# A diffusion backbone's split matmuls: leading in one weight panel row block by row block instead of two

## The chip, the cores and the metric

The kernel runs on one NeuronCore of a Trainium2 chip, as one program. The metric is the device time of one execution in microseconds (us), as the median of several runs; lower is better. Five engines run side by side, each with its own instruction stream: TensorE (PE, matmuls), VectorE (DVE), ScalarE (ACT), GpSimd (POOL) and SyncE (SP), which here only starts DMA transfers. They wait for each other on semaphores.

## The reference

A backbone of four layers runs over 256 latent tokens and 256 context tokens with 1024 features. Each layer has another token mixer (latent attention, Hyena, S5, FNet), followed by a SwiGLU with 2816 hidden features. Before each of them the stream is normalised and modulated; this gives the matmul's input h. The parts that matter here:

```python
def rmsnorm(x, g):
    xf = x.astype(jnp.float32)
    y = xf * lax.rsqrt(jnp.mean(jnp.square(xf), axis=-1, keepdims=True) + NORM_EPS)
    return (y * g.astype(jnp.float32)).astype(x.dtype)

def modulate(h, shift, scale):
    return h * (1.0 + scale) + shift

def swiglu(h, w13, w2):
    a, b = jnp.split(h @ w13, 2, axis=-1)
    return (jax.nn.silu(a) * b) @ w2
...
    for i in range(DEPTH):
...
        hl = modulate(rmsnorm(xl, mix_pre_g[i]), mod_l[0], mod_l[1])
...
        xl = xl + mod_l[2] * rmsnorm(yl, mix_post_g[i])
        hl = modulate(rmsnorm(xl, ffn_pre_g[i]), mod_l[3], mod_l[4])
        xl = xl + mod_l[5] * rmsnorm(swiglu(hl, ffn_w13[i], ffn_w2[i]), ffn_post_g[i])
```

The first matmul of the attention is `h_lat @ w_in` (1024 to 1088 columns, of which the last 64 are the shared rotary key), the first of Hyena is `h @ w_in` (1024 to 3072). Layers 0 and 1 work on 512 tokens (latent and context), the feed-forwards of layers 2 and 3 on 256.

## The kernel before

**Split matmuls.** Features lie on partitions, in KD = 8 row blocks of 128; tokens lie along the free dimension. To keep accuracy, each operand is split in a rounded part (hi) and a remainder (lo), and `product` issues three matmuls for one block: hi x hi (L935), lo of h x hi of w (L936), hi of h x lo of w (L937). A weight comes in panels of 256 columns, 1 MB each; a panel's two column chunks of 128 are called q = 0 and 1. For one panel and 8 blocks that is 2 x 8 x 3 = 48 matmuls.

**Panels.** `Split` handles them. SP loads panel p into one of two ring slots (`sp_issue`, L213), as soon as panel p - 2 has been split completely. ScalarE rounds a panel in two halves of four blocks (`round`, L892: w_hi <- ring), VectorE forms the remainder of each half (`remain`, L897: w_lo <- ring, w_hi). `nth_split(i, j)` says which count of the semaphore `w_split_ready` means that half j of panel i is there; TensorE waits for it at blocks 0 and 4 (`wait`). w_hi and w_lo hold two panels, so panel 2 overwrites panel 0.

**The join and the lead-in.** Between two stages a `Join` adds the stage's result to the stream x and forms the next input, block by block. VectorE: `normed` (L707), `scaled` (L697, a later block), `update` (L702), `remainder` (L711, which gives h_lo and is the last step of a block). ScalarE between them: shift and scale (L681), rounding to h_hi (L685). A join marked `parts=True` in front of a split matmul knows it as `first`, and does the first panels' rounding and remainders inside its own loop. TensorE follows with `lead_in` (L917): for each block k it waits for h_lo of block k and then multiplies it into all accumulators (PSUM banks) in its list `outs`. Before the change the list has panels 0 and 1, four accumulators of 512 or 256 columns, 12 matmuls for a block; in the attention panel 0 and the 64 rotary columns (panel 1), 9 matmuls. In the middle of the lead-in `w_stepped` tells ScalarE that the first half of w_hi may be overwritten with panel 2.

After the lead-in the panels from 2 on run one after another, panel by panel, each chunk through all eight blocks. Between panels stand pieces of the modulation (`mods.tensor`, L397): matmuls of another weight that is streamed through a ring of two 1 MB slots; SP refills it (L360) in the same queue as the panels.

There are six lead-ins: attention (Mla, from 54 us), feed-forward of layer 0 (468 us), Hyena (872 us), feed-forward of layer 1 (1216 us), and of layers 2 and 3 (2168 and 2446 us, 256 columns). Everything is ordered by hand; no scheduler moves instructions.

## Time and profile before

| | |
|---|---|
| time, median of 3 runs | 2664.7 us (2653.64 to 2664.8) |
| the profiled execution's own time | 2662.34 us |
| its span, first to last instruction | 2660.5 us |
| mean granted TensorE clock | 0.895 of full |
| TensorE busy | 2243.5 us (84%) |
| VectorE busy | 1200.3 us (45%) |
| ScalarE busy | 791.3 us (30%) |
| HBM read | 295.12 MB |

The profile is of one execution. PE stands for matmuls and PEld for weight loads, which overlap them. The recorded length of a matmul includes its way through the array, so that successive ones overlap; what counts is the distance of their starts. The chain is found backwards from the last instruction. A timeline gives start, length, engine, line, operation and tiles (output first), a count, and in brackets how long the engine had stood idle and what ended that.

### The profile page before, as it was taken

To read this page: it belongs to the slowest core of one execution; us is meant where nothing else is said; L and a number is where in the kernel's file an instruction comes from. 1 tells how busy PE (TensorE), PEld (TensorE's weight loads), DVE (VectorE), ACT (ScalarE), POOL (GpSimd) and SP (SyncE) were. 2 spreads that over 40 slices of the span, in tenths; PEclk is the share of its full clock that TensorE was granted. 3 is DMA by queue.
4 is the path that set the end of the run, shared out by engine and by line. 5 is a ranking of instruction groups with operands and counts; after the bars stand their busy time and mean duration, and the time that the engine had idled before them with its cause. 6 is when DMAs were issued, how large, how long until landed. Compare 5 with 4: busy or idle time off the path is not lost.

```text
span 2660.5 us, 31449 instructions
## 1 busy us (share of the span) xinstructions
PE 2243.5 (84%) x13211; PEld 1741.3 (65%) x13211; DVE 1200.3 (45%) x1939; ACT 791.3 (30%) x1293; POOL 169.4 (6%) x139
## 2 busy tenths in 40 slices
PE   4998879999999899898999995352653789988998
PEld 3664446777777675456777774242643779977998
DVE  2223333522333764515322336876576145553554
ACT  2441113422224422124222224110110144443544
POOL 0000000000000001000000001550640000000000
PEclk8997889999999999999999997675665799999999
DMA  6243321343333444213545434010010335532553
GB/s 231 96 166 135 103 79 32 127 139 123 135 138 115 159 159 141 88 48 102 183 159 190 158 127 113 23 26 0 9 32 0 81 122 189 188 106 95 175 189 112
DMA packets 226311, 305.52 MB, mean 115 GB/s; under 512 B 8598, under 2 KB 197729, under 8 KB 225852
## 3 DMA queue, kind: packets, MB, share of 16 engines
q1 hardware_dynamic: 223840, 298.22, 33.2%
q0 software_dynamic: 1616, 5.05, 0.8%
q8 instruction: 104, 1.70, 0.3%
q10 hardware_dynamic: 716, 0.26, 0.0%
q14 instruction: 35, 0.29, 0.0%
HBM read 295.12 MB, written 4.19 MB: 113 GB/s over the span
## 4 chain that ended last, share of the span: by engine, by line
PE 73%; DVE 18%; ACT 4%; DMA 2%; issue 2%; SPq 1%; POOL 0%; DVEq 0%; ACTq 0%
PE bank L935 17%; PE bank L936 16%; PE bank L937 16%; PE bank L397 4%; PE bank L801 3%; PE bank L846 2%; ACT arena L681 2%; PE bank L1653 1%; DVE arena L707 1%; PE bank L2207 1%; PE bank L2209 1%; PE bank L2208 1%; DVE h_lo L711 1%; ACT h_hi L685 1%; PE bank L2167 1%
## 5 line engine op out<-in xcount | busy, mean ns | idle before, releaser
L935 PE MATMUL bank<-h_hi,w_hi 128*128 128x512 f32 (+1 forms) x1480 | 514.6, 348 | 31.6 <-DVE h_lo L711 30.5
L936 PE MATMUL bank<-h_lo,w_hi 128*128 128x512 f32 (+1 forms) x1480 | 506.8, 342 | 0.0
L937 PE MATMUL bank<-h_hi,w_lo 128*128 128x512 f32 (+1 forms) x1480 | 505.5, 342 | 0.0
L897 DVE TENSOR_TENSOR w_lo<-ring,w_hi 128x1024 fp32r<-128x1024 f32 (+1 forms) x282 | 323.6, 1186 | 387.3 <-ACT w_hi L892 387.2
L935 PEld LDWEIGHTS bank<-h_hi,w_hi 128*128 128x128 f32 x1480 | 283.8, 192 | 86.7 <-DVE h_lo L711 41.4
L892 ACT ACTIVATE w_hi<-ring 128x1024 fp32r<-128x1024 f32 (+1 forms) x282 | 274.5, 1019 | 117.0 <-PE bank L937 115.0
L937 PEld LDWEIGHTS bank<-h_hi,w_lo 128*128 128x128 f32 x1480 | 283.8, 192 | 32.4 <-issue 0.2
L936 PEld LDWEIGHTS bank<-h_lo,w_hi 128*128 128x128 f32 x1480 | 283.9, 192 | 29.6 <-issue 0.2
L935 PE MATMUL bank<-g_hi,w_hi 128*128 128x512 f32 (+1 forms) x704 | 241.1, 343 | 0.0
L936 PE MATMUL bank<-g_lo,w_hi 128*128 128x512 f32 (+1 forms) x704 | 237.2, 337 | 0.0
L937 PE MATMUL bank<-g_hi,w_lo 128*128 128x512 f32 (+1 forms) x704 | 236.6, 336 | 0.0
L2207 PE MATMUL bank<-arena 128*128 128x32 f32 x128 | 39.3, 401 | 133.1 <-DVE arena L2127 133.1
L935 PEld LDWEIGHTS bank<-g_hi,w_hi 128*128 128x128 f32 x704 | 133.4, 190 | 26.3 <-issue 10.0
L937 PEld LDWEIGHTS bank<-g_hi,w_lo 128*128 128x128 f32 x704 | 133.6, 190 | 14.3
L936 PEld LDWEIGHTS bank<-g_lo,w_hi 128*128 128x128 f32 x704 | 133.6, 190 | 12.9
L1068 DVE TENSOR_TENSOR arena<-arena,bank 128x512 f32<-128x512 f32 (+1 forms) x88 | 48.3, 553 | 175.3 <-PE bank L937 173.0
L2207 PEld LDWEIGHTS bank<-arena 128*128 128x128 f32 x128 | 34.9, 332 | 133.3 <-issue 133.3
L1049 ACT ACTIVATE g_hi<-arena 128x512 fp32r<-128x512 f32 (+1 forms) x88 | 45.9, 525 | 252.8 <-DVE arena L1068 252.7
L2167 PE MATMUL bank<-ident,arena 128*128 128x128 f32 x128 | 28.6, 398 | 95.3 <-DVE arena L2043 95.3
L1043 ACT ACTIVATE arena<-bank 128x512 f32<-128x512 f32 (+1 forms) x88 | 42.7, 490 | 216.5 <-PE bank L937 215.2
L397 PE MATMUL bank<-mod_ring,silu_c 128*32 128x256 f32 x1408 | 97.8, 399 | 5.5 <-DMA mod_ring<-mod_w 5.5
L2167 PEld LDWEIGHTS bank<-ident,arena 128*128 128x128 f32 x128 | 22.8, 206 | 97.4 <-issue 48.9
(329 smaller groups left out, 3345.8 us busy)
## 6 DMA issues: line engine op xcount, KB each, us to landing
ring<-ffn_w SPq DMA_DIRECT2D x120, 1024.0 KB, 5.1
mod_ring<-mod_w SPq DMA_DIRECT2D x88, 1024.0 KB, 7.2
ring<-ffn_w SPq DMA_DIRECT2D x16, 768.0 KB, 4.4
ring<-hy_w_in SPq DMA_DIRECT2D x12, 1024.0 KB, 5.2
arena<-mod_w SPq DMA_DIRECT2D x8, 1024.0 KB, 17.5
ring<-s_w_glu SPq DMA_DIRECT2D x8, 1024.0 KB, 5.4
ring<-mla_w_uq SPq DMA_DIRECT2D x8, 576.0 KB, 4.2
ring<-mla_w_in SPq DMA_DIRECT2D x4, 1024.0 KB, 7.1
```

Source lines behind the costliest of these rows:

```text
L397: last = nc.tensor.matmul(MODB[32 * g:32 * g + 32, 0:256], silu_c[:, k, :], self.slot(m)[:, kk, 256 * g:256 * g + 256], start=(k == 0), st ...
L681: last = nc.scalar.activation(dst, src, ACT.Identity, bias=mod.shift(f > 1, k, s), scale=mod.factor(f, k, s))
L801: last = nc.tensor.matmul(self.banks[c % 4][:, 0:self.n], v[:, kl, q * P:(q + 1) * P], self.rhs(k), start=(k == 0), stop=(k == self.kk - 1))
L846: last = nc.tensor.matmul(self.bank(c, t)[:, 0:self.n], v[:, k, q * P:(q + 1) * P], self.rhs(k), start=(k == 0), stop=(k == KD - 1))
L892: nc.scalar.activation(self.hi[:, i % SPLIT, a:b], self.w.slot(i)[:, a:b], ACT.Copy).then_inc(w_rounded, 1)
L897: nc.vector.tensor_tensor(self.lo[:, i % SPLIT, a:b], self.w.slot(i)[:, a:b], self.hi[:, i % SPLIT, a:b].bitcast(F32), ALU.subtract).then_ ...
L935: nc.tensor.matmul(o, w[0], v[0], start=first, stop=False)
L936: nc.tensor.matmul(o, w[0], v[1], start=False, stop=False)
L937: return nc.tensor.matmul(o, w[1], v[0], start=False, stop=last)
L1068: nc.vector.tensor_tensor(self.silus[:, q, 0:n], self.silus[:, q, 0:n], self.out(i, q)[:, 0:n], ALU.mult).then_inc(ffn_product, 1)
L2167: last = nc.tensor.transpose(bank[q][:, j * P:(j + 1) * P], self.pw[:, 2 * q + j // 2, j % 2, :], ident[:, :])
L2207: nc.tensor.matmul(o, self.m0[:, gh, :], self.u[:, g, 0:CH], start=True, stop=False)
```

## The change

In each of the six places only panel 0 is led in block by block, over two accumulators (6 matmuls for a block). Panel 1 follows behind the lead-in in the usual order: chunk by chunk, each through all blocks. In the join, VectorE forms panel 1's two remainders no longer behind blocks 0 and 2 but behind block 7, and `nth_split` counts the halves in their plain order. ScalarE's roundings stay where they were. The modulation piece that belongs to panel 1 now stands behind panel 1.

```diff
--- before.py
+++ after.py
@@ -753,12 +753,11 @@
                         update(k + 1)
                     if self.parts:
                         remainder(k)
-                        if k == 0:
-                            self.first.remain(dve, 1, 0)
                         if k == 2:
                             self.first.remain(dve, 0, 1)
+                        if k == KD - 1:
+                            self.first.remain(dve, 1, 0)
                             self.first.remain(dve, 1, 1)
-                        if k == KD - 1:
                             self.first.remain(dve, 2, 0)
 
 
@@ -870,8 +869,6 @@
 
             def nth_split(self, i, j):
 
-                if self.stepped and i < 2:
-                    return 2 * self.s0 + 2 * j + i + 1
                 return 2 * (self.s0 + i) + j + 1
 
             def halves(self, i):
@@ -991,11 +988,10 @@
 
             def tensor(self, pe):
                 n = self.n
-                lead_in(pe, self.w, self.pre, [(i, q, self.out(i, q)[:, 0:n]) for i in range(2) for q in range(2)], ffn_summed)
+                lead_in(pe, self.w, self.pre, [(i, q, self.out(i, q)[:, 0:n]) for i in range(1) for q in range(2)], ffn_summed)
                 mods.tensor(pe, (self, 0))
-                mods.tensor(pe, (self, 1))
                 for i, (kind, part, kk, c) in enumerate(self.plan):
-                    if i < 2:
+                    if i < 1:
                         continue
                     hi, lo = self.w.parts(i)
                     for q in range(2):
@@ -1164,11 +1160,11 @@
                 pool.dma_start(self.turn[0:ROPE], A["k_turn"]).then_inc(self.loaded, 16)
 
             def tensor(self, pe):
-                lead_in(pe, self.win, self.pre, [(0, 0, bank[0][:, :]), (0, 1, bank[1][:, :]), (1, 0, bank[2][0:ROPE, :])], self.z_summed)
-                for n in range(3):
+                lead_in(pe, self.win, self.pre, [(0, 0, bank[0][:, :]), (0, 1, bank[1][:, :])], self.z_summed)
+                for n in range(2):
                     mods.tensor(pe, (self, "in", n))
                 for n, (c, i) in enumerate(zip(self.order, self.panel)):
-                    if n < 3:
+                    if n < 2:
                         continue
                     m = ROPE if c == 8 else P
                     hi, lo = self.win.parts(i)
@@ -1566,10 +1562,9 @@
                     rhs = self.zt[0:EMB, :] if r == 0 else self.a[0:WIDTH, :]
                     nc.tensor.matmul(bank[5][0:WIDTH, 0:LAT], lhs, rhs, start=True, stop=True).then_inc(self.f_summed, 1)
 
-                lead_in(pe, self.win, self.pre, [(c // 2, c % 2, self.out(c)[:, :]) for c in range(4)], self.u_summed)
+                lead_in(pe, self.win, self.pre, [(c // 2, c % 2, self.out(c)[:, :]) for c in range(2)], self.u_summed)
                 mods.tensor(pe, (self, "in", 0))
-                mods.tensor(pe, (self, "in", 1))
-                for c in range(4, 24):
+                for c in range(2, 24):
                     if c in self.SINES:
                         if c == self.SINES[0]:
                             pe.wait_ge(self.u_moved, 6)
```

On TensorE, in the feed-forward of layer 0, around the first block of the lead-in. Before (the banks are the accumulators; h_split_ready is the wait for h_lo of a block):

```order
L935 MATMUL bank1<-h_hi_51,w_hi_52 128x512
L936 MATMUL bank1<-h_lo_56,w_hi_52 128x512
L937 MATMUL bank1<-h_hi_51,w_lo_53 128x512
L935 MATMUL bank2<-h_hi_51,w_hi_52 128x512 [waits w_split_ready]
L936 MATMUL bank2<-h_lo_56,w_hi_52 128x512
L937 MATMUL bank2<-h_hi_51,w_lo_53 128x512
L935 MATMUL bank3<-h_hi_51,w_hi_52 128x512
L936 MATMUL bank3<-h_lo_56,w_hi_52 128x512
L937 MATMUL bank3<-h_hi_51,w_lo_53 128x512
L935 MATMUL bank0<-h_hi_51,w_hi_52 128x512 [waits h_split_ready]
```

and now:

```order
L934 MATMUL bank0<-h_hi_51,w_lo_53 128x512
L932 MATMUL bank1<-h_hi_51,w_hi_52 128x512
L933 MATMUL bank1<-h_lo_56,w_hi_52 128x512
L934 MATMUL bank1<-h_hi_51,w_lo_53 128x512
L932 MATMUL bank0<-h_hi_51,w_hi_52 128x512 [waits h_split_ready]
L933 MATMUL bank0<-h_lo_56,w_hi_52 128x512
L934 MATMUL bank0<-h_hi_51,w_lo_53 128x512
L932 MATMUL bank1<-h_hi_51,w_hi_52 128x512
```

The six matmuls into bank2 and bank3 no longer stand between block 0 and block 1. At the end of the same lead-in TensorE now has, where before bank2 and bank3 of block 7, the modulation and then panel 2 (bank4) stood:

```order
L932 MATMUL bank1<-h_hi_51,w_hi_52 128x512
L933 MATMUL bank1<-h_lo_56,w_hi_52 128x512
L934 MATMUL bank1<-h_hi_51,w_lo_53 128x512
L932 MATMUL bank2<-h_hi_51,w_hi_52 128x512 [waits w_split_ready]
L933 MATMUL bank2<-h_lo_56,w_hi_52 128x512
L934 MATMUL bank2<-h_hi_51,w_lo_53 128x512
L932 MATMUL bank2<-h_hi_51,w_hi_52 128x512
L933 MATMUL bank2<-h_lo_56,w_hi_52 128x512
L934 MATMUL bank2<-h_hi_51,w_lo_53 128x512
```

Panel 1's run into bank2 and then bank3, 48 matmuls, begins behind the last block. On VectorE in the join before that feed-forward, before (w_lo is a weight remainder, h_lo that of a block, arena_50 the join's scratch; the line numbers are those of each file):

```order
L897 TENSOR_TENSOR w_lo_53<-ring,w_hi_52 128x1024 [waits w_rounded]
L711 TENSOR_TENSOR h_lo_56<-arena_50,h_hi_51 128x512 [waits h_rounded]
L897 TENSOR_TENSOR w_lo_53<-ring,w_hi_52 128x1024 [waits w_rounded]
L707 TENSOR_TENSOR arena_50<-x_sb,bank4 128x512 [waits x_updated]
L697 TENSOR_TENSOR arena_50<-arena_50,bank5 128x512
L702 TENSOR_TENSOR x_sb<-x_sb,arena_50 128x512 [waits join_step]
L711 TENSOR_TENSOR h_lo_56<-arena_50,h_hi_51 128x512 [waits h_rounded]
L707 TENSOR_TENSOR arena_50<-x_sb,bank4 128x512 [waits x_updated]
L697 TENSOR_TENSOR arena_50<-arena_50,bank5 128x512
L702 TENSOR_TENSOR x_sb<-x_sb,arena_50 128x512 [waits join_step]
L711 TENSOR_TENSOR h_lo_56<-arena_50,h_hi_51 128x512 [waits h_rounded]
L897 TENSOR_TENSOR w_lo_53<-ring,w_hi_52 128x1024 [waits w_rounded] x2
```

and now:

```order
L894 TENSOR_TENSOR w_lo_53<-ring,w_hi_52 128x1024 [waits w_rounded]
L711 TENSOR_TENSOR h_lo_56<-arena_50,h_hi_51 128x512 [waits h_rounded]
L707 TENSOR_TENSOR arena_50<-x_sb,bank4 128x512 [waits x_updated]
L697 TENSOR_TENSOR arena_50<-arena_50,bank5 128x512
L702 TENSOR_TENSOR x_sb<-x_sb,arena_50 128x512 [waits join_step]
L711 TENSOR_TENSOR h_lo_56<-arena_50,h_hi_51 128x512 [waits h_rounded]
L707 TENSOR_TENSOR arena_50<-x_sb,bank4 128x512 [waits x_updated]
L697 TENSOR_TENSOR arena_50<-arena_50,bank5 128x512
L702 TENSOR_TENSOR x_sb<-x_sb,arena_50 128x512 [waits join_step]
L711 TENSOR_TENSOR h_lo_56<-arena_50,h_hi_51 128x512 [waits h_rounded]
L894 TENSOR_TENSOR w_lo_53<-ring,w_hi_52 128x1024 [waits w_rounded]
L707 TENSOR_TENSOR arena_50<-x_sb,bank4 128x512 [waits x_updated]
```

One weight remainder behind block 0 and one behind block 2 are gone. Behind block 7, before:

```order
L711 TENSOR_TENSOR h_lo_56<-arena_50,h_hi_51 128x512 [waits h_rounded]
L707 TENSOR_TENSOR arena_50<-x_sb,bank4 128x512 [waits x_updated]
L711 TENSOR_TENSOR h_lo_56<-arena_50,h_hi_51 128x512 [waits h_rounded]
L897 TENSOR_TENSOR w_lo_53<-ring,w_hi_52 128x1024 [waits w_rounded] x2
L1068 TENSOR_TENSOR arena_50<-arena_50,bank2 128x512 [waits ffn_silu,ffn_summed]
L1068 TENSOR_TENSOR arena_50<-arena_50,bank3 128x512 [waits ffn_silu,ffn_summed]
L1084 TENSOR_TENSOR g_lo_55<-arena_50,g_hi_54 128x512 [waits ffn_g_rounded] x2
```

and now:

```order
L711 TENSOR_TENSOR h_lo_56<-arena_50,h_hi_51 128x512 [waits h_rounded]
L707 TENSOR_TENSOR arena_50<-x_sb,bank4 128x512 [waits x_updated]
L711 TENSOR_TENSOR h_lo_56<-arena_50,h_hi_51 128x512 [waits h_rounded]
L894 TENSOR_TENSOR w_lo_53<-ring,w_hi_52 128x1024 [waits w_rounded] x4
L1064 TENSOR_TENSOR arena_50<-arena_50,bank2 128x512 [waits ffn_silu,ffn_summed]
L1064 TENSOR_TENSOR arena_50<-arena_50,bank3 128x512 [waits ffn_silu,ffn_summed]
L1080 TENSOR_TENSOR g_lo_55<-arena_50,g_hi_54 128x512 [waits ffn_g_rounded] x2
```

Two more of them stand behind the last h_lo: panel 1's two, ahead of panel 2's first half.

## Rows read from the trace of the kernel before

**Rows 1.** The page: TensorE's busy time and its clock in 40 slices.
```profile
PE 2243.5 (84%) x13211; PEld 1741.3 (65%) x13211; DVE 1200.3 (45%) x1939; ACT 791.3 (30%) x1293; POOL 169.4 (6%) x139
...
PEclk8997889999999999999999997675665799999999
```

**Rows 2.** The page's chain that ended last: by engine, by line.
```profile
PE 73%; DVE 18%; ACT 4%; DMA 2%; issue 2%; SPq 1%; POOL 0%; DVEq 0%; ACTq 0%
PE bank L935 17%; PE bank L936 16%; PE bank L937 16%; PE bank L397 4%; PE bank L801 3%; PE bank L846 2%; ACT arena L681 2%; PE bank L1653 1%; DVE arena L707 1%; PE bank L2207 1%; PE bank L2209 1%; PE bank L2208 1%; DVE h_lo L711 1%; ACT h_hi L685 1%; PE bank L2167 1%
```

**Rows 3.** Waits: who for whom, total us, times, longest.
```profile
PE bank L935 <- DVE h_lo L711: 36.4, 25, 3.9
```

**Rows 4.** Timelines of ScalarE and VectorE, feed-forward 0's lead-in.
```profile
477.81 1.09 ACT L681 ACTIVATE arena<-arena,modv,affine 128x256 f32<-128x256 f32 x2 [3.63 <-DVE arena L707]
...
488.93 0.69 DVE L711 TENSOR_TENSOR h_lo<-arena,h_hi 128x512 fp32r<-128x512 f32 x1 [0.50 <-ACT h_hi L685]
...
492.05 0.69 DVE L711 TENSOR_TENSOR h_lo<-arena,h_hi 128x512 fp32r<-128x512 f32 x1 [1.83 <-ACT h_hi L685]
```

**Rows 5.** Timeline of TensorE, the same lead-in.
```profile
480.34 0.53 PE L935 MATMUL bank<-h_hi,w_hi 128*128 128x512 f32 x1 [2.37 <-DVE h_lo L711]
480.67 0.62 PE L936 MATMUL bank<-h_lo,w_hi 128*128 128x512 f32 x1
...
483.66 0.59 PE L937 MATMUL bank<-h_hi,w_lo 128*128 128x512 f32 x1
...
492.97 0.39 PE L935 MATMUL bank<-h_hi,w_hi 128*128 128x512 f32 x1
...
495.46 0.39 PE L937 MATMUL bank<-h_hi,w_lo 128*128 128x512 f32 x1
```

**Rows 6.** Timelines of SP and TensorE, behind Hyena's lead-in.
```profile
905.07 0.58 SPq L360 DMA_DIRECT2D mod_ring<-mod_w  x1
...
915.98 1.07 PE L397 MATMUL bank<-mod_ring,silu_c 128*32 128x256 f32 x16 [2.81 <-DMA mod_ring<-mod_w]
```

**Rows 7.** Timeline of VectorE, the attention's lead-in.
```profile
53.80 0.42 DVE L897 TENSOR_TENSOR w_lo<-ring,w_hi 128x256 fp32r<-128x256 f32 x1
54.14 0.68 DVE L707 TENSOR_TENSOR arena<-x_sb,bank 128x512 f32<-128x512 f32 x1
```

**Rows 8.** Timelines of VectorE and TensorE, end of feed-forward 2's lead-in.
```profile
2184.04 1.22 DVE L897 TENSOR_TENSOR w_lo<-ring,w_hi 128x1024 fp32r<-128x1024 f32 x1
...
2186.91 0.28 PE L936 MATMUL bank<-h_lo,w_hi 128*128 128x256 f32 x1
2187.03 0.28 PE L937 MATMUL bank<-h_hi,w_lo 128*128 128x256 f32 x1
2187.56 0.39 PE L935 MATMUL bank<-h_hi,w_hi 128*128 128x256 f32 x1 [0.26 <-DVE w_lo L897]
```

**Rows 9.** The chain in order of time, feed-forward 0: start, us, what.
```profile
474.90 2.27 DVE w_lo L897 x2
```

**Rows 10.** SP's timeline and DMA issues (median to landing), feed-forward 2.
```profile
2173.63 1.50 SPq L213 DMA_DIRECT2D ring<-ffn_w  x2
...
ring<-ffn_w SPq DMA_DIRECT2D x2, 1024.0 KB, 6.5
```

**Rows 11.** Busy us by stretch, PE first; behind POOL, the granted clock.
```profile
231.00:405.00 174.00, 139.84 (x651) 81.77 (x652) 70.93 (x215) 28.10 (x98) 0.00 (x0) 0.76 0.29 97
...
480.67:484.08 3.41, 3.41 (x9) 2.63 (x8) 2.88 (x6) 1.78 (x4) 0.00 (x0) 0.50 0.83 277
```

**Rows 12.** Timeline of TensorE: the shortest and longest of the other five pauses.
```profile
2176.66 0.39 PE L935 MATMUL bank<-h_hi,w_hi 128*128 128x256 f32 x1 [1.57 <-DVE h_lo L711]
2176.89 0.28 PE L936 MATMUL bank<-h_lo,w_hi 128*128 128x256 f32 x1
2177.01 0.28 PE L937 MATMUL bank<-h_hi,w_lo 128*128 128x256 f32 x1
...
2455.30 0.39 PE L935 MATMUL bank<-h_hi,w_hi 128*128 128x256 f32 x1 [2.45 <-DVE h_lo L711]
```

## The prediction, written before the changed kernel ran

> **What bounds the kernel now.** I read the page first. TensorE is busy for 84% of the span and its granted clock is full except in a few slices [rows 1]. The chain that ended last runs along TensorE for 73% of the span, and three lines of it, the three products of a split matmul (L935 to L937), hold half of the span alone [rows 2]. So an edit is worth what it does to the moment at which TensorE gets past a place, unless another engine stands in front of TensorE there. The waits say where one does: matmuls of L935 waited 36.4 us for the block remainders of L711 [rows 3]. All of these lie in the six lead-ins, where a stage's activations arrive block by block. Then I read the timelines of the lead-ins, VectorE beside TensorE. In the feed-forward of layer 0, h_lo blocks come 3.12 us apart on VectorE (488.93, then 492.05) [rows 4]. TensorE's twelve matmuls of a block start 0.226 us apart (492.97 to 495.46, eleven steps) and take 2.7 us [rows 5]. So 2.7 of every 3.12 us in the loop are matmul work that has to be done anyway: the lead-in hides it. The last block ends at 492.74 (492.05 plus 0.69) and TensorE takes it at 492.97, so TensorE is 0.2 us behind there, and only 12 matmuls are left.
>
> **The change, part by part.** It touches six places: the lead-ins of the four feed-forwards, of the latent attention and of Hyena.
>
> 1. TensorE. None of its matmuls is added or removed, but six instead of twelve stand between two blocks, and panel 1's 48 follow as one run. Behind the last block stood 12 matmuls, now 6 + 48 = 54: 42 more that used to lie under VectorE's loop. Nothing covers them, since panel 2 stands behind them in TensorE's order. For 512 columns 42 x 0.226 = 9.5 us, plus 0.1 for the slower start of a run behind a wait (480.34 to 480.67 is 0.33): +9.6. For 256 columns the steps are 0.12 (2186.91 to 2187.03) [rows 8]: 42 x 0.12 + 0.1 = +5.1. In the attention panel 1 is one chunk of 64 columns: before 9 matmuls after the last block, now 6 + 24, 21 x 0.228 + 0.1 = +4.9.
>
> 2. VectorE. Two weight remainders leave the loop (behind block 0 and behind block 2) and stand behind block 7. A pair takes 2.27 us on the chain, from start to next start [rows 9], that is 1.14 each. ScalarE waits for VectorE's L707 after both places, behind block 2 for 3.63 us [rows 4], so the loop of the two engines shortens by what VectorE drops: the last block comes 2.27 us earlier. In the attention the two are 128x256, and the next instruction starts 0.34 after one [rows 7]: -0.7. At the end TensorE needs the first of them for panel 1. It starts 0.08 before the block's end, as the pair in the loop does, runs 1.22, and so ends 1.1 us after the block. TensorE's six last matmuls cover that at 512 columns (1.5 us), but not at 256 (0.8 us): +0.3 there. The second one is needed 12 matmuls later, 2.7 or 1.4 us, and is ready.
>
> 3. Waits that panel 1 now covers. In Hyena the third modulation panel waited 2.81 us for its DMA [rows 6]. TensorE comes there 7 us later and the load, issued at 905.07 before, is not later, since SP waits for panel 2's remainder, which GpSimd's setup (it waits for the last h_lo) and not panel 1 sets: -2.8. In the narrow feed-forwards panel 2's fifth block waited for its remainder: it started 0.53 after its forerunner instead of 0.12 [rows 8]: -0.4 each.
>
> 4. SP. Panel 3's load waits for panel 1's second remainder, now behind block 7, about 8 to 10 us later. A load takes 5 to 6.5 us, and two that used to start together shared the queue [rows 10]. TensorE needs panel 3 only after panels 1 and 2, 11.5 us behind the last block even at 256 columns, and rounding and remainder of a panel cost 2.0 + 2.4 us. For 256 columns: remainder at +2.4, landed at +8, but rounding must wait for panel 1 anyway (+6.7), done at +12. That is tight: nothing by the sum, up to 1 us each in two stages. Refills of the modulation ring behind it have over 10 us. Panel 2's load is freed 1.1 us earlier, and ScalarE reaches its rounding 2.3 earlier; it had no wait for it before, and now the load is alone on the queue. Nothing, bound 0.5 a stage.
>
> The sum, in us of TensorE's arrival at panel 2 or behind its wait:
> attention 4.9 - 0.7 = 4.2; feed-forward 0: 9.6 - 2.3 - 0.2 (it was behind) = 7.1 [rows 5]; Hyena 9.6 - 2.3 - 2.8 = 4.5; feed-forward 1: 9.6 - 2.3 = 7.3; feed-forwards 2 and 3: 5.1 - 2.3 + 0.3 - 0.4 = 2.7 each. Together 28.5 us. After a lead-in TensorE has no wait to give it back in, so all of it reaches the end.
>
> **The clock** is the term that the trace does not show for the new form. In feed-forward 0 the granted clock fell from 2.4 to 1.2 GHz after TensorE had stood still for 2.37 us. The starts were then 0.427 apart, eight of them [rows 5], and the stretch shows 0.50 [rows 11]. Now TensorE works 1.5 us and stands still 1.6 us in every block, eight times. In the blocks themselves a low clock costs nothing: six starts at 0.427 are 2.6 us of 3.12. It costs only if it is low where panel 1 begins: up to 8 x 0.2 = 1.6 us a stage. The ends are 0 and 6 x 1.6 = 10. Each lead-in has one such pause, and one in six brought a fall (the other five, 1.57 to 2.45 us long, had none; after the shortest the 256-column starts stay 0.12 apart, 2176.89 to 2177.01) [rows 12], but repeated pauses are nearer to attention's slices, where the mean is 0.76 [rows 11]. I take a third, 3 us.
> The Trainium skill speaks for this edit here: "TensorE: Matmul & The Clock Gate", section "Loop structure matters more than you think", wants all k-steps of one output tile back to back. Panel 1 now has that form. By that page it would gain; the trace shows the same spacing in both forms at full clock, 0.12 at 256 columns interleaved over four accumulators [rows 12] and 0.12 within one, panel 2's [rows 8], so the sum would stay as it is, and I go by the row.
>
> 28.5 + 3 = 31.5. Against the profiled execution of 2662.3 us (span 2660.5) that is 2693.8; I say 2694. The median of the runs shown, 2664.7, is 2.4 above the profiled one, and the lowest, 2653.6, is 9 below, which the range has to take in.
>
> **Rivals.**
> - The clock swings between its levels in every lead-in. For it: pauses as long as the work, in every block. Against it: five of the six single pauses left it alone. It gives 28.5 + 10, about 2701. The Trainium skill describes such a case, the same page, section "A second HAM failure mode: psum-queue depth-cycling": short idles between groups make the clock go up and down. By it this rival's time holds; no row here shows the new pattern.
> - Late weights: panel 3 comes late because its slot is freed behind block 7. Against it: item 4. If rounding and remainder cannot catch up, 1 us in each of six stages and a late modulation panel in Hyena: 2662.3 + 28.5 + 3 + 9 = 2703.
> - Nothing is lost, because another engine sets these places: then TensorE's later arrival would hide behind a wait. Only the waits of item 3 could do that, and they are in the sum. The same time would come out if panel 1 stayed interleaved, but the order shows it moved. 2662.
> - Faster. TensorE's later arrival puts the attention's heads elsewhere against the clock's changes. From 231 to 405 us the mean clock is 0.76 [rows 11], so it is low for 2 x 0.24 x 174 = 84 us. If all of that were granted in full, at most 42 us would come back, more than the 28.5 lost: 2649. It decides from 42 us gained to be over 0.5% faster, that is only if every low stretch goes. Half of it would need no less than a change in what feeds the heads, and nothing does that. A part, 10 us in either direction, is well possible, and it may be what parts the runs of 2653.6 and 2664.8.
>
> **How the numbers follow.** The forecast, 2687 to 2700: 0.64. Swinging clock around 2701: 0.13. Late weights 2703 and more: 0.04. Attention's clock gives 10 us or so back, 2678 to 2686: 0.09. No loss, within 0.5%: 0.07. Faster: 0.03. A measurement of this kernel can tell about 0.5% (13 us) from no change. Slower by over 0.5%, above 2678, gets 0.90, the same 0.07, faster 0.03. For the range I take the lowest run plus the sum, 2653.6 + 28.5 = 2682, and at the top the swinging clock with some lateness, 2704.
>
> **What would show it.** Right: the last h_lo of a lead-in comes 2.3 us earlier (0.7 in attention); TensorE waits about 1.6 us for L711 before almost every block, so that L935's wait for L711 in all grows from 36.4 us to some 80; 48 matmuls of panel 1 follow the last block and panel 2 starts 7 us later against it in the wide feed-forwards; Hyena's modulation wait is gone. Wrong: if the granted clock is 0.5 at the start of panel 1 in most stages, the term of 3 was too small. If h_lo does not come earlier, ScalarE and not VectorE sets the loop, and each stage loses 2.3 more (2706). If panel 3's first matmul waits for w_lo, item 4 failed.

## The result, and the profile after

| | before | after |
|---|---|---|
| time, median of 4 runs each | 2660.53 us (2653.64 to 2664.8) | 2687.46 us (2685.76 to 2691.07) |
| the profiled execution's own time | 2662.34 us | 2685.94 us |
| its span | 2660.5 us | 2684.1 us |
| mean granted TensorE clock | 0.895 | 0.893 |

The changed kernel is slower: the ratio is 1.0106, with a 95% interval from 1.0076 to 1.0135, that is 20 to 36 us. The forecast was 2694, 31.5 us above the profiled execution of before, with a range of 2682 to 2704. The measured 2687 lies in it, 26.9 us above the median of before; the four runs of before are the three shown ahead of the prediction and a fourth of 2656.36 us.

The page of the changed kernel answers [rows 1] and [rows 2]. TensorE's three products now stand in L932 to L934; the count, 13211 matmuls in all, is as before. On the chain that ended last TensorE has 74% instead of 73.

```profile
PE 2249.3 (84%) x13211; PEld 1742.6 (65%) x13211; DVE 1200.5 (45%) x1939; ACT 791.9 (30%) x1293; POOL 169.4 (6%) x139
...
PEclk8997889999999999999999998675665789998999
...
PE 74%; DVE 17%; ACT 4%; DMA 2%; issue 2%; SPq 1%; DVEq 0%; ACTq 0%
```

The wait for h_lo, from the view of waits, answers [rows 3] (who waits for whom, us in total, times, longest): 48 waits instead of 25, eight in each of six lead-ins.

```profile
PE bank L932 <- DVE h_lo L711: 59.1, 48, 3.9
```

VectorE's timeline in the lead-in of feed-forward 0 answers [rows 4]. Blocks still come 3.12 us apart, and behind the last one all four weight remainders stand as one run.

```profile
484.61 0.69 DVE L711 TENSOR_TENSOR h_lo<-arena,h_hi 128x512 fp32r<-128x512 f32 x1 [0.50 <-ACT h_hi L685]
...
487.73 0.69 DVE L711 TENSOR_TENSOR h_lo<-arena,h_hi 128x512 fp32r<-128x512 f32 x1 [1.82 <-ACT h_hi L685]
488.33 4.62 DVE L894 TENSOR_TENSOR w_lo<-ring,w_hi 128x1024 fp32r<-128x1024 f32 x4
```

TensorE there answers [rows 5]. It waits 1.45 us for the last block, works six matmuls, goes on to panel 1 at 489.96 without a wait, comes out at 500.95 (48 matmuls later) and begins panel 2 at 501.95, 14.2 us behind the start of the last h_lo. Before, the last h_lo started at 492.05 and panel 2 at 496.78, 4.7 us behind it. The first line is that one, from the timeline of before; the others are of the changed kernel.

```profile
496.78 0.50 PE L935 MATMUL bank<-h_hi,w_hi 128*128 128x512 f32 x1
```

```profile
486.62 0.40 PE L934 MATMUL bank<-h_hi,w_lo 128*128 128x512 f32 x1
488.47 0.49 PE L932 MATMUL bank<-h_hi,w_hi 128*128 128x512 f32 x1 [1.45 <-DVE h_lo L711]
...
489.96 0.40 PE L932 MATMUL bank<-h_hi,w_hi 128*128 128x512 f32 x1
...
500.63 0.39 PE L934 MATMUL bank<-h_hi,w_lo 128*128 128x512 f32 x1
500.95 1.07 PE L397 MATMUL bank<-mod_ring,silu_c 128*32 128x256 f32 x16
501.95 0.50 PE L932 MATMUL bank<-h_hi,w_hi 128*128 128x512 f32 x1
```

Behind Hyena's lead-in the third modulation piece no longer waits for its DMA, which answers [rows 6]:

```profile
925.76 1.07 PE L397 MATMUL bank<-mod_ring,silu_c 128*32 128x256 f32 x16
```

In feed-forward 2 the end of the lead-in looks other than in [rows 8] and [rows 12]. The starts are 0.21 us apart until 2200.80 and 0.12 after it. The busy times by stretch (first the length, then each engine's busy time, behind POOL the granted clock) show the low level, 0.50, through the narrow lead-ins and into panel 1:

```profile
2198.92 0.58 PE L932 MATMUL bank<-h_hi,w_hi 128*128 128x256 f32 x1 [0.23 <-DVE h_lo L711]
...
2200.37 0.41 PE L932 MATMUL bank<-h_hi,w_hi 128*128 128x256 f32 x1
2200.58 0.40 PE L933 MATMUL bank<-h_lo,w_hi 128*128 128x256 f32 x1
2200.80 0.30 PE L934 MATMUL bank<-h_hi,w_lo 128*128 128x256 f32 x1
2200.93 0.28 PE L932 MATMUL bank<-h_hi,w_hi 128*128 128x256 f32 x1
```

```profile
2184.00:2198.45 14.45, 11.28 (x42) 9.47 (x42) 10.96 (x28) 8.91 (x16) 0.00 (x0) 0.50 0.22 73
2198.45:2201.50 3.05, 2.82 (x16) 2.58 (x15) 3.05 (x4) 0.89 (x1) 0.00 (x0) 0.61 0.02 5
...
2480.20:2483.20 3.00, 2.77 (x13) 2.50 (x12) 2.98 (x4) 0.81 (x1) 0.00 (x0) 0.50 0.00 0
```

The most useful reading of all traces is the distance from the first h_lo of one lead-in to the first of the next, taken from VectorE's timelines (L711). It cuts the kernel in six pieces and shows where time goes. The last column but one is a part of the first piece: the time from the first to the last of the 32 remainders that VectorE makes in the attention's heads. The last is the granted clock from 266 to 400 us, where the heads run. The rows named e are the experiments below.

| us | attention | feed-fwd 0 | Hyena | feed-fwd 1, layer 2 | feed-fwd 2, layer 3 | feed-fwd 3 to the end | heads | clock 266 to 400 |
|---|---|---|---|---|---|---|---|---|
| before | 413.65 | 404.23 | 344.55 | 951.53 | 278.63 | 214.72 | 140.24 | 0.82 |
| before again (e8) | 402.69 | 404.26 | 346.12 | 951.80 | 278.67 | 214.83 | 128.59 | 0.91 |
| after | 411.79 | 411.44 | 348.94 | 958.79 | 281.76 | 218.36 | 132.95 | 0.86 |
| e1 | 414.43 | 414.50 | 351.16 | 963.99 | 283.00 | 221.11 | 134.83 | 0.86 |
| e5 | 417.78 | 411.44 | 347.25 | 958.79 | 281.31 | 217.84 | 140.24 | 0.83 |
| e6 | 405.62 | 409.24 | 347.94 | 957.42 | 280.48 | 216.48 | 131.77 | 0.89 |
| e3 | 396.90 | 402.80 | 341.04 | 950.42 | 277.26 | 212.61 | 128.30 | 0.92 |
| e9 | 395.20 | 401.16 | 342.72 | 950.24 | 277.22 | 212.69 | 128.50 | 0.91 |
| e11 | 398.27 | 401.93 | 337.29 | 950.04 | 278.06 | 212.22 | 131.37 | 1.00 |
| e4 | 409.47 | 406.88 | 344.64 | 956.61 | 282.06 | 216.07 | 137.33 | 0.83 |
| e10 | 405.91 | 404.19 | 346.09 | 951.82 | 278.57 | 214.44 | 131.37 | 1.00 |
| e12 | 409.29 | 411.41 | 349.58 | 960.64 | 282.21 | 218.66 | 131.37 | 1.00 |

### The profile page after: what moved, and what is told of

Same layout as the page of the kernel before. It is cut to its first block, busy times and chain, and to the rows that moved or that the text cites. A ratio compares the mean times of both kernels' runs of the same rounds, so it can differ in the third digit from the quotient of the medians.

```text
span 2684.1 us, 31449 instructions
## 1 busy us (share of the span) xinstructions
PE 2249.3 (84%) x13211; PEld 1742.6 (65%) x13211; DVE 1200.5 (45%) x1939; ACT 791.9 (30%) x1293; POOL 169.4 (6%) x139
## 4 chain that ended last, share of the span: by engine, by line
PE 74%; DVE 17%; ACT 4%; DMA 2%; issue 2%; SPq 1%; DVEq 0%; ACTq 0%
PE bank L932 17%; PE bank L933 17%; PE bank L934 17%; PE bank L397 4%; PE bank L800 3%; PE bank L845 2%; ACT arena L681 2%; PE bank L1648 1%; DVE arena L707 1%; PE bank L2202 1%; PE bank L2204 1%; PE bank L2203 1%; DVE h_lo L711 1%; ACT h_hi L685 1%; PE bank L2162 1%
## 5 line engine op out<-in xcount | busy, mean ns | idle before, releaser
L932 PE MATMUL bank<-h_hi,w_hi 128*128 128x512 f32 (+1 forms) x1480 | 520.2, 351 | 45.2 <-DVE h_lo L711 45.2
L934 PE MATMUL bank<-h_hi,w_lo 128*128 128x512 f32 (+1 forms) x1480 | 509.5, 344 | 0.0
L932 PEld LDWEIGHTS bank<-h_hi,w_hi 128*128 128x128 f32 x1480 | 286.8, 194 | 105.4 <-DVE h_lo L711 61.6
L934 PEld LDWEIGHTS bank<-h_hi,w_lo 128*128 128x128 f32 x1480 | 287.5, 194 | 32.5
L932 PE MATMUL bank<-g_hi,w_hi 128*128 128x512 f32 (+1 forms) x704 | 241.1, 343 | 0.0
L934 PE MATMUL bank<-g_hi,w_lo 128*128 128x512 f32 (+1 forms) x704 | 236.6, 336 | 0.0
L932 PEld LDWEIGHTS bank<-g_hi,w_hi 128*128 128x128 f32 x704 | 133.5, 190 | 26.3 <-issue 10.0
L934 PEld LDWEIGHTS bank<-g_hi,w_lo 128*128 128x128 f32 x704 | 133.6, 190 | 14.4
L2162 PE MATMUL bank<-ident,arena 128*128 128x128 f32 x128 | 28.2, 393 | 94.8 <-DVE arena L2038 94.8
L932 PE MATMUL bank<-h_hi,hy_w_hi 128*128 128x512 f32 x192 | 77.5, 404 | 14.0 <-DVE h_lo L711 14.0
```

The lines of the kernel that those rows point to most:

```text
L932: nc.tensor.matmul(o, w[0], v[0], start=first, stop=False)
L934: return nc.tensor.matmul(o, w[1], v[0], start=False, stop=last)
L2162: last = nc.tensor.transpose(bank[q][:, j * P:(j + 1) * P], self.pw[:, 2 * q + j // 2, j % 2, :], ident[:, :])
```

## The experiments

### The TensorE side alone (e1)

The changed kernel, with VectorE's order and the counting of before:

```diff
                     if self.parts:
                         remainder(k)
+                        if k == 0:
+                            self.first.remain(dve, 1, 0)
                         if k == 2:
                             self.first.remain(dve, 0, 1)
-                        if k == KD - 1:
-                            self.first.remain(dve, 1, 0)
                             self.first.remain(dve, 1, 1)
+                        if k == KD - 1:
                             self.first.remain(dve, 2, 0)
...
+                if self.stepped and i < 2:
+                    return 2 * self.s0 + 2 * j + i + 1
                 return 2 * (self.s0 + i) + j + 1
```

> Only the TensorE side of the change: one panel is led in, panel 1 follows as one run, but VectorE forms panel 1's two remainders inside the loop again (behind blocks 0 and 2). My theory is that VectorE sets the loop, so what it drops comes back in full: the last h_lo of a wide lead-in comes 2.3 us later than in the changed kernel (0.7 in the attention), and the whole takes 5 x 2.27 + 0.7 = 12 us more than the changed kernel: 2699 us, that is +39 against before. The rival is that ScalarE sets the loop and VectorE's order does not matter: then 2687 us, within 3 us of the changed kernel, and the last h_lo stands where it stood.

Measured: 2704.61 us (2696.29 to 2705.76), 1.0171 of before (1.0146 to 1.0196), 17 us above the changed kernel. From its first to its last h_lo a wide lead-in takes 25.18 us, the attention 23.59 and a narrow one 16.54; the changed kernel has 22.92, 22.92 and 14.47, the kernel before 25.2, 23.6 and 16.55. VectorE's timeline in feed-forward 0 shows the pair of weight remainders that stands in the way:

```profile
475.70 0.69 DVE L711 TENSOR_TENSOR h_lo<-arena,h_hi 128x512 fp32r<-128x512 f32 x1 [0.50 <-ACT h_hi L685]
476.31 2.35 DVE L897 TENSOR_TENSOR w_lo<-ring,w_hi 128x1024 fp32r<-128x1024 f32 x2
478.58 0.68 DVE L707 TENSOR_TENSOR arena<-x_sb,bank 128x512 f32<-128x512 f32 x1
...
481.08 0.69 DVE L711 TENSOR_TENSOR h_lo<-arena,h_hi 128x512 fp32r<-128x512 f32 x1 [0.49 <-ACT h_hi L685]
```

VectorE's order sets the loop, to the tenth of a us, and the rival (ScalarE) falls. In feed-forward 0 TensorE reaches the modulation piece behind panel 1 38.4 us after the first h_lo, the changed kernel 36.1: the 2.3 us arrive there in full. The total went over the expected 12 in other places. The heads drew 134.83 us instead of 132.95. In the piece of feed-forward 1 and layer 2, e1 stands 5.2 us above the changed kernel instead of 2.3; some 2.5 of them arise between 1650 and 2140 us, in layer 2's mixer, whose code is the same, and e12, the changed kernel's own code there, stands 1.85 above it in the same piece. So these are not the edit's.

### The change in the attention alone (e2)

```diff
-                lead_in(pe, self.win, self.pre, [(0, 0, bank[0][:, :]), (0, 1, bank[1][:, :]), (1, 0, bank[2][0:ROPE, :])], self.z_summed)
-                for n in range(3):
+                lead_in(pe, self.win, self.pre, [(0, 0, bank[0][:, :]), (0, 1, bank[1][:, :])], self.z_summed)
+                for n in range(2):
```

with the new order of the weight remainders and the plain counting for this stage only.

> The change in the attention's lead-in alone; the other five stages lead in two panels as before. My theory, from the two traces: TensorE leaves the attention's lead-in and latent projections 4 us later, the heads behind it fall differently against the clock and give about 6 us back, so the feed-forward's first h_lo comes 2 us earlier than before and the whole takes 2 us less than before. The rival is the plain sum: what is lost in a lead-in is never given back, the whole takes 4.2 us more, and the 6 us were the luck of one execution.

Measured: 2661.34 us (2659.07 to 2672.95, 10 runs) against 2658.53 (17 runs): 1.0021 (1.0003 to 1.0038), 0.8 to 10 us more. The plain sum, 4.2, lies in it, a gain of 2 does not. Yet in its profiled execution the attention's piece (53 to 467 us in the profile of before) is 4.1 us shorter than in the profile of before, 409.51 against 413.65, since the heads took 131.68 us instead of 140.24. The two would agree if the profile of before had been a poor draw, which the next two runs look at.

### A delay in front of the heads (e7), and before once more (e8)

```diff
+                hi, lo = self.win.parts(0)
+                for _ in range(18):
+                    nc.tensor.matmul(bank[3][:, :], hi[:, 0, 0:P], h_hi[:, 0, :], start=True, stop=True)
                 for n in range(3):
                     mods.tensor(pe, (self, "in", n))
```

> The kernel before with 18 matmuls of 512 columns that nobody reads (4.1 us) behind the attention's lead-in, so that all that follows starts 4.1 us later. In the profiled executions of the changed kernel and of the one with the change in the attention alone, the attention's heads (266 to 400 us) gave 6.7 and 7.7 us back. If a shift does that by moving the heads against the clock, this kernel gives as much back: the whole takes 2 to 4 us less than before. If those were differences between one execution and another, the whole takes 4.1 us more: 2663 against 2659.

> The kernel before, unchanged, profiled a second time. If the heads' time differs from one execution to another of one kernel, the stretch between the first h_lo of the attention and that of the first feed-forward (53.19 to 466.84, 413.65 us in the first profile) comes out several us shorter or longer, while every other stretch repeats within 0.5 us. If the heads' time is set by where they stand, it repeats too.

Measured: e7 2663.93 us (2654.84 to 2670.77, 10 runs) against 2660.78, a ratio of 1.0011 (0.9991 to 1.003): between 2.4 us less and 8 more, so it holds the 4.1 of the sum and just reaches the 2 less of the other theory. e8 decides. It took 2654.39 us in the profiled execution, and its heads took 11.65 us less than those of the first profile. In the table every other piece repeats within 0.3 us, but for Hyena (1.6). The granted clock between 266 and 400 us goes with it; first the kernel before, then the same kernel again:

```profile
266.00:400.00 134.00, 109.47 (x554) 64.56 (x553) 51.23 (x167) 24.05 (x84) 0.00 (x0) 0.82 0.28 91
```

```profile
266.00:400.00 134.00, 108.29 (x608) 67.15 (x607) 58.38 (x184) 29.10 (x94) 0.00 (x0) 0.91 0.29 94
```

The same two executions, each from the first to the last remainder of its heads:

```profile
266.32:406.56 140.24, 115.80 (x581) 70.52 (x582) 54.62 (x178) 25.59 (x91) 0.00 (x0) 0.81 0.26 86
```

```profile
267.91:396.50 128.59, 102.98 (x581) 63.02 (x582) 54.42 (x179) 25.54 (x91) 0.00 (x0) 0.91 0.29 93
```

TensorE records 581 matmuls in both. They keep it busy for 115.80 and 102.98 us, and it stands still for 24.4 and 25.6. So the longer heads have no longer waits: the same matmuls take 12.8 us more at the lower clock. One unchanged kernel differs by 11 us from execution to execution, in the heads, by its clock. A single pair of profiles can't weigh 4 us in front of them.

Hyena's 1.6 us are the clock's too. Behind the wait for its DMA the third modulation piece, which took 1.07 us in the first profile [rows 6], takes 1.94 in e8 (whose lines are numbered one higher):

```profile
906.12 1.94 PE L398 MATMUL bank<-mod_ring,silu_c 128*32 128x256 f32 x16 [2.98 <-DMA mod_ring<-mod_w]
```

e2, e7 and e10, which have the Hyena of before, repeat e8's piece within 0.1 us (346.15, 346.18 and 346.09). The first profile, 344.55, is the odd one of the five.

### The heads' pauses filled (e10)

```diff
                     mods.tensor(pe, (self, "unit", u))
+                    if u < n - 1:
+                        for _ in range(3):
+                            nc.tensor.matmul(bank[2 + (u + 1) % 2][:, 0:2 * P], ident[:, :], self.kn[:, 0, 0:2 * P], start=True, stop=True)
```

> The kernel before with three matmuls of 256 columns that nobody reads at the end of each of 31 units of the attention's heads, where TensorE waits. The first feed-forward's h_lo came 413.65 us behind the attention's in one profile of the kernel before and 402.69 in another, with a clock of 0.82 and 0.91 between 266 and 400 us, and all else repeated within 1.6 us. If the clock in the pauses is the reason, it is now near 1.00 there, the distance is 400 to 403 us and the runs of this kernel lie within 5 us instead of 17, at 2653 us. The rival is that the pauses are too short for them: three take some 0.5 us, 31 x 0.5 = 15 us more, 2675 us.

Measured: 2654.16 us (2652.04 to 2658.28, 10 runs), 0.998 of before (0.9966 to 0.9993). The kernel before has its 13 runs beside it over 13.5 us, this one its 10 over 6.2. The clock of the stretch and the fillers in TensorE's timeline:

```profile
266.00:400.00 134.00, 131.05 (x770) 89.16 (x769) 55.80 (x181) 26.38 (x91) 0.00 (x0) 1.00 0.28 91
```

```profile
301.27 1.56 PE L1294 MATMUL bank<-arena,ident 128*128 128x256 f32 x6
302.67 0.38 PE L1270 MATMUL bank<-ident,arena 128*128 128x128 f32 x2
```

The three fillers take 1.4 us from start to next start (301.27 to 302.67), not the 0.5 that I had put down, and still the heads are done in 131.37 us, 2.8 more than the better unfilled execution and 8.9 less than the first profile. The distance between the two first h_lo is 405.91 us, not the 400 to 403 expected. TensorE is busy for 131.05 of the 134 us, so its own work, fillers included, all but sets the time there, and the even time alone would not prove the clock. The two executions of the unfilled kernel do, with the same matmuls and nearly the same waits at two clocks. What makes the clock fall more in one execution than in another stays open.

### The change with the heads held (e12)

The changed kernel with the filler of e10.

> The changed kernel with the filled heads of e10. With the heads held at full clock the difference to e10 is the cost of the change without the heads' chance. By the distances of the stages in the traces it is 4.1 (attention), 7.2, 4.4 (or 2.8, against the second profile of before), 7.3, 3.1 and 3.6 us, 28 to 30 together: 2683 us, and the profiled distance from the attention's first h_lo to the first feed-forward's is 4.1 us longer than e10's 405.9. The rival is that the later start gives time back in the heads even at full clock: 2677 us or less.

Measured: 2685.17 us (2684.96 to 2687.62, 5 runs), 1.0098 of before (1.0078 to 1.0118). Against e10's 2654.16 that is 31.0 us, from two chips (the medians of before beside them are 2662.16 and 2660.76), and 30.8 between the two spans (2685.8 and 2655.0). The heads take 131.37 us in both, to the hundredth, so a later start gives nothing back at full clock. By the table the change costs 3.4 in the attention, 7.2 in feed-forward 0, 3.5 in Hyena, 8.8 in the piece of feed-forward 1 (7.3 in the first profile of the changed kernel; most of the 1.5 more arises in layer 2's mixer, between 1950 and 2110 us, where nothing was changed), 3.6 and 4.2.

### The pauses of the lead-ins filled (e5)

The changed kernel, in `lead_in`:

```diff
                 if k == KD // 2 - 1:
                     last.then_inc(w_stepped, 1)
+                if k < KD - 1:
+                    for _ in range(5 if n == TOK else 8):
+                        nc.tensor.matmul(spare, h_hi[:, k, 0:P], h_hi[:, k, 0:n], start=True, stop=True)
```

> The changed kernel with matmuls that nobody reads in TensorE's pauses of the lead-in: five of 512 columns behind each of blocks 0 to 6 of a wide lead-in, eight of 256 columns in a narrow one (11 x 0.226 = 2.5 us of 3.12, 14 x 0.12 = 1.7 of 2.07 at full clock). They write the accumulators of panel 1 before its first product overwrites them. My theory is that the pauses hold the clock down (0.50 in both narrow lead-ins and 0.60 and 0.50 in the 3 us behind the last h_lo) and that this costs about 0.5 and 1 us where panel 1 begins in the narrow stages, and nothing in the wide ones: with the pauses filled the clock behind the last h_lo is 1.00 everywhere and the whole takes 1 to 2 us less than the changed kernel, 2686 us. The rival is that the low clock in the lead-ins costs much more, the 3 us of my prediction and above: 2684 us or less. If the clock is low when a lead-in begins, eleven matmuls take 4.7 us and the filling itself costs: 2690 us.

Measured: 2686.65 us (2685.32 to 2689.92), the ratio 1.0087 (1.006 to 1.0114) beside 1.0106 of the changed kernel: no difference that these runs could show. The pieces are sharper. Its clock in the 3 us behind the last h_lo is 1.00 in both narrow stages (here feed-forward 2), where the changed kernel had 0.61 and 0.50:

```profile
2188.95:2203.38 14.43, 13.95 (x94) 13.95 (x95) 10.97 (x27) 8.92 (x16) 0.00 (x0) 0.78 0.22 74
2203.40:2206.40 3.00, 2.84 (x23) 2.63 (x22) 3.00 (x4) 1.51 (x2) 0.00 (x0) 1.00 0.00 0
```

and the pieces are 0.45 and 0.52 us shorter there, 0.00 in both wide feed-forwards, and 1.7 in Hyena, which is as much as Hyena differs by between two executions of before. The attention outside its heads is 1.3 shorter, but e12, which has the changed kernel's lead-ins, is 0.9 shorter there too. So the two narrow stages show about 1 us that the low clock of the lead-ins cost, and the rest is within what one kernel differs by. My 3 was too much, the swinging clock's 10 far too much.

The 1 us is a net figure. At full clock six matmuls no longer cover panel 1's first remainder, and TensorE waits for it, in both narrow stages (L935 to L937 are the products in e5):

```profile
2205.00 0.39 PE L935 MATMUL bank<-h_hi,w_hi 128*128 128x256 f32 x1 [0.16 <-DVE w_lo L894]
```

It starts 0.44 us after its forerunner (2204.56) instead of 0.12. That is the 0.3 of item 2, which the changed kernel, at half clock there, did not pay.

### Half the change (e6)

```diff
-                lead_in(pe, self.w, self.pre, [(i, q, self.out(i, q)[:, 0:n]) for i in range(2) for q in range(2)], ffn_summed)
+                lead_in(pe, self.w, self.pre, [(i, q, self.out(i, q)[:, 0:n]) for i, q in ((0, 0), (0, 1), (1, 0))], ffn_summed)
...
-                lead_in(pe, self.win, self.pre, [(c // 2, c % 2, self.out(c)[:, :]) for c in range(4)], self.u_summed)
+                lead_in(pe, self.win, self.pre, [(c // 2, c % 2, self.out(c)[:, :]) for c in range(3)], self.u_summed)
```

> Half the change: in the four feed-forwards and Hyena panel 0 and the first chunk of panel 1 are led in (three accumulators, nine matmuls for a block), and only the second chunk of panel 1 (24 matmuls) follows as a run. VectorE keeps the order of before, the attention is as before. If each matmul that stands behind the last block instead of under the loop costs its own length and nothing else, 33 instead of 12 stand there: 21 x 0.226 = 4.8 us in a wide stage, 21 x 0.12 = 2.5 in a narrow one, less the modulation wait of 2.8 in Hyena, 0.4 in each narrow stage and 0.2 in the first feed-forward: 4.6 + 2.0 + 4.8 + 2.1 + 2.1 = 15.6 us more than before, 2675 us. The rival is that pauses cost by themselves (the clock, a restart at each block), so that most of the loss comes with the first pauses: +22 us or more, 2681. The last h_lo of each lead-in stands as in the kernel before (25.2 and 16.55 us behind the first).

Measured: 2670.82 us (2666.43 to 2678.28, 10 runs), 1.0035 of before (1.0018 to 1.0052), that is 5 to 14 us more: the expected 15.6 lies just above. By the table it costs 5.0, 3.4 (1.8 against e8), 5.9, 1.9 and 1.8 us in the five stages that it touches, 16 to 18 together. The steps are near the expected ones, and the rival of a large first pause (22 us or more) falls by either measure. The timed difference, 10 us by the medians, 12.4 by the lowest runs and 6.8 by the highest, is smaller than the sum of the pieces. The heads' scatter is of that size, but that it is the reason was not shown.

### A quicker loop, with two panels (e3, e9) and with one (e4)

VectorE's order in the loop, on the kernel before (e3) and on the changed one (e4):

```diff
                 for k in range(KD):
-                    normed(k)
+                    if k == 0 or not self.parts:
+                        normed(k)
                     if k == 0 and self.first:
                         self.first.remain(dve, 0, 0)
-                    if self.post and k:
+                    if self.parts:
+                        if k + 1 < KD:
+                            normed(k + 1)
+                        if self.post:
+                            scaled(k + 2)
+                            update(k + 2)
+                    elif self.post and k:
                         scaled(k + 1)
                         update(k + 1)
                     if self.parts:
                         remainder(k)
```

> The kernel before (two panels led in) with another order of VectorE in the loop: L707 of the next block and L697 and L702 of the one behind it stand ahead of this block's remainder L711, so that ScalarE works on block k+1 while VectorE finishes block k. If the 3.12 us of a block are one round through both engines (0.6 for L707, 1.7 on ScalarE, 0.6 for L711 and the handovers), the distance falls to VectorE's own four steps, about 2.56 us, where TensorE's twelve matmuls of 2.7 us bound it: about 3.3 us less in each of three wide stages, 2.5 in the two narrow ones, 6 in the attention (VectorE has only two steps there, ScalarE 1.8 us, TensorE's nine matmuls 2.05): 21 us less than before, 2640 us. The rival is that TensorE or ScalarE sets the distance already: within 3 us of before.

> The changed kernel (one panel led in) with the same other order in the loop. My theory: the 42 matmuls behind the last block cost the same whatever the loop's speed, so against the pipelined kernel with two panels it loses 6.5 us in a wide feed-forward, 3.7 in Hyena, 2.5 in a narrow one and 3.2 in the attention, 25 us together: 2665 us, about the kernel before. The rival: with a faster loop TensorE's twelve matmuls become the bound in the two-panel form, so that one panel fits better: no more than 10 us behind the two-panel form, 2650 us.

Measured: e3 2635.74 us (2632.12 to 2642.9), 0.9923 of before (0.9897 to 0.9948). e4 2666.46 us (2659.17 to 2672.85, 8 runs), 1.0032 (1.0014 to 1.005), 31 us above e3. VectorE of e3 has no wait left and gives a block every 2.53 us:

```profile
461.94 0.69 DVE L711 TENSOR_TENSOR h_lo<-arena,h_hi 128x512 fp32r<-128x512 f32 x1
462.55 0.68 DVE L707 TENSOR_TENSOR arena<-x_sb,bank 128x512 f32<-128x512 f32 x1
463.14 0.68 DVE L697 TENSOR_TENSOR arena<-arena,bank 128x512 f32<-128x512 f32 x1
463.86 0.69 DVE L702 TENSOR_TENSOR x_sb<-x_sb,arena 128x512 f32<-128x512 f32 x1
464.47 0.69 DVE L711 TENSOR_TENSOR h_lo<-arena,h_hi 128x512 fp32r<-128x512 f32 x1
```

The waits say who is late. In e3 (products in L942) TensorE waits for h_lo 13 times, 27.7 us in all, in e4 (L939) 26 times, 44.9 us:

```profile
PE bank L942 <- DVE h_lo L711: 27.7, 13, 4.4
```

```profile
PE bank L939 <- DVE h_lo L711: 44.9, 26, 4.4
```

The total came out as expected, its parts did not. The feed-forward pieces shrank by 1.4, 1.1, 1.4 and 2.1 us instead of 3.3 and 2.5, since more of VectorE's steps now stand ahead of the first remainder. Counted from the reciprocal of r_post that opens a join (458.38 in feed-forward 0 of before, with its first h_lo at 466.84), that remainder comes 1.5 us later in feed-forward 0, 1.9 in Hyena and 1.0 to 1.2 in the other three; the 1.95 of e9's expectation is near Hyena's and no other's. The attention shrank by 16.8 instead of 6, most of it in the heads (128.30 instead of 140.24); against e8, whose heads drew about the same, by 5.8. So the total of the first profiles was met by a good draw in the heads. In e4 the heads drew 137.33, which is 9 of the 31 us. The rival (one panel fits a faster loop better) falls either way: e4 stands 3.5 to 6.2 us above e3 in each of the other five pieces.

e9 moved L697 and L702 behind the remainder, to get the first block out sooner, and of the weight remainders behind block 2 one behind block 3:

```diff
+                    if self.parts and k + 1 < KD:
+                        normed(k + 1)
...
                     if self.parts:
                         remainder(k)
...
+                        if self.post:
+                            scaled(k + 2)
+                            update(k + 2)
```

> Two panels led in, the pipelined loop of e3 with one step moved: the remainder L711 of block k stands right behind L707 of block k+1, and L697 and L702 behind it; of panel 1's and panel 0's second weight remainders one each stands behind blocks 2 and 3. In e3 the first h_lo came 1.95 us later than in the kernel before, which took back over half of the 3.4 us of a wide stage. If that is the reason, the first h_lo comes 1.2 us earlier in a wide stage and 0.7 in a narrow one, TensorE's twelve matmuls per block still bound the rest, and the whole takes 5 us less than e3 (1.2 x 3 + 0.7 x 2), that is 27 less than before: 2633 against 2660. The attention has no L697 and L702 and stays as in e3. The rival is that TensorE, which is behind by the first, low-clocked block anyway, hides an earlier start: as e3, 2638.

Measured: 2637.67 us (2634.48 to 2648.09), 0.9929 (0.9904 to 0.9954), as e3. The time is the rival's, but not for its reason. From first to last h_lo a wide lead-in now takes 21.2 us instead of 19.2, and still TensorE comes out earlier. In feed-forward 0 the modulation piece behind the lead-in stands 34.3 us behind the same reciprocal instead of 35.5, in Hyena 34.4 instead of 36.0, and feed-forward 0's piece is 1.6 us shorter (401.16). In Hyena it is lost again: the piece is 1.7 us longer (342.72), since the third modulation piece now waits 2.02 us for its DMA instead of 0.80 and runs at a low clock behind the wait:

```profile
890.77 1.72 PE L397 MATMUL bank<-mod_ring,silu_c 128*32 128x256 f32 x16 [2.02 <-DMA mod_ring<-mod_w]
```

The profiled execution is 2.4 us shorter than e3's by its span, the median 1.9 longer; the four runs of each can't part the two kernels.

### The version that beats both (e11)

e3's loop and e10's filler together.

> e3 (two panels led in, pipelined loop) and the filled heads of e10 together, as a version that should beat both kernels. e3 was 22.8 us faster than before and e10 6.6. If they touch different things both count: 27 to 29 us less than before, 2632 against 2660, with a clock of 1.00 from 266 to 390 us and the runs within 7 us. The rival is that e3's heads already had the better clock and that the 10 us which the attention gave beyond its lead-in are the same gain: 22 us less, 2638.

Measured: 2633.93 us (2633.59 to 2636.15, 6 runs), 0.9906 of before (0.9888 to 0.9923), 20 to 30 us less than before and some 50 less than the changed kernel. Its heads take 131.37 us, 3 more than e3's profiled execution had by chance. It stands between the two expectations, 2632 and 2638. By the medians of its own chip it is 28.2 us below before, where e3 was 22.8 on another; the interval holds both 22 and 28, so these runs don't say whether the two gains add up. The medians of e3 and e11 differ by 1.8 us only, and the runs of e11 lie over 2.6 us instead of 10.8.

## Why the prediction was right

The direction, the mechanism and the size held. Between e10 and e12, where the heads don't scatter, the change costs 31.0 us; the forecast said 31.5. That the two agree so closely is partly luck: the forecast is 28.5 of work and waits and 3 of clock. The clock cost about 1. Layer 2's mixer added 1.5 in e12 that is not the change's, and the last two stages cost 0.9 and 1.5 more than summed, clock included, while the attention and Hyena cost 0.8 and 1.0 less.

**1. TensorE, 42 more matmuls behind the last block.** Right. In feed-forward 0 panel 2 starts 14.2 us behind the last h_lo instead of 4.7. The 9.5 us between them are 42 times 0.226. e6 with 21 of the 42 costs 5.0 where 42 cost 7.2 together with VectorE's 2.3 back.

**2. VectorE, 2.3 us back per stage, 0.7 in the attention.** Right. From first to last h_lo: 25.21 to 22.92, 23.61 to 22.92, and 16.55 to 14.47 in the narrow stages, where 0.2 is missing (a block came 2.07 after another instead of 1.88). e1 took the 2.3 away again. TensorE found the remainders of panel 1 ready: none of its waits there names w_lo. In the wide stages that was forecast. In the narrow ones the forecast had 0.3 us for it, which e5 shows at full clock.

**3. Covered waits.** Right in kind: Hyena's 2.81 us wait is gone. TensorE reaches that piece 49.5 us behind the first h_lo (925.76 less 876.25) instead of 44.9, 4.6 later, as summed (4.5). The piece between the stages grew by 4.4 against the first profile of before, but by 2.8 against the second and 3.5 from e10 to e12. In four of the five executions of the old Hyena the clock fell at the wait for the DMA, which made the piece 1.6 us longer, and the change takes away this wait. The prediction counted the pauses that the change makes, and not the clock behind the one that it removes.

**4. SP.** Right: panel 3 was never late; TensorE has no wait for w_lo there.

**The sum** by pieces of the first pair of profiles, measured against forecast: 7.2 (7.1), 4.4 (4.5), 7.3 (7.3), 3.1 (2.7), 3.6 (2.7). The lead-in of the attention gave 4.1 (4.2): the modulation piece that stood at 86.9 us stands at 90.9, and the stage began 0.2 earlier.

**The clock term, 3 us,** was the mis-sized step. My reasoning held that a low clock costs nothing as long as the blocks wait and has its price where panel 1 begins; the four wide stages all began panel 1 at full clock, only the two narrow ones began it low. The term measured 1.0 (e5). What I did not foresee is its shape: in the narrow lead-ins the clock did not swing, it stayed at 0.50 from the first block to the last. In the wide ones it did swing: feed-forward 0's waits between blocks are 0.2 and 0.7 us where blocks ran at the low level and 1.45 where they ran at the full. That cost nothing, since six matmuls at half speed (2.6 us) still fit between two blocks. The Trainium skill ("TensorE: Matmul & The Clock Gate", "A second HAM failure mode: psum-queue depth-cycling") describes a clock that goes up and down under short idles and speaks of throughput lost to it. The attention's heads are such a place in this kernel (e8's stretches of 20 us from 290 on have 0.83, 1.00, 0.83 and 1.00). The wide lead-ins have the swing without the loss: e5 filled their pauses, and the pieces of feed-forwards 0 and 1 stayed at 411.44 and 958.79 us.

**The waits.** I expected L935's 36.4 us to grow to some 80, it is 59.1: in the wide stages the pauses are the expected 1.4 to 1.5 where the clock was full (2.6 behind the weight remainder of block 2), but only 0.2 to 0.7 where it was low. In the narrow ones, at half clock throughout, six matmuls take twice as long and leave 0.2 to 0.4 (1.4 behind the weight remainder).

**Why 2687 and not 2694.** The base was the profiled execution of before, whose heads took 140.24 us. The changed kernel's took 132.95. That is 7.3 us by chance. Outside the heads the attention's piece grew by 5.4 (4.1 in the lead-in, the rest just ahead of the heads) and the other five by 25.6 together, and 2662.3 + 31.0 - 7.3 = 2686.0; the profiled time is 2685.94. I had written that 10 us in either direction were possible there and might part the runs of before, which e8 showed; but I called it an effect of TensorE's later arrival. With the heads filled, e12 showed none, and e7, which moved the unfilled heads by 4 us, gave no gain that its runs could show.

**The rivals.** Swinging clock: e5, 1 us instead of 10. Late weights: no wait. Nothing lost: the pieces. Faster by the attention's clock: it did not come. e10, with all of the heads at full clock, gains 6.6 us and not 42; but its fillers take TensorE's time themselves, so no run shows the heads at full clock without them.

## What to carry to other kernels

A loop in which TensorE waits for each block is free room: count the matmuls that fit in a block's distance, and each one that is moved out costs its full length at the end (0.226 us here for 512 columns at full clock). What the order of the weights gave back was less: 2.3 of 9.5 us. Before costing an edit against one profile, cut two profiles of the same unchanged kernel into pieces between the same marks; a piece that doesn't repeat (here 11 us in the heads) can't carry an argument of 4 us. And look at the round trip of the loop itself: letting ScalarE work on the next block while VectorE finishes this one took 23 us off the kernel before and, by the medians of two chips, 21 off the changed one.
